# Expert stage of a decoder block: half of the second tile's row sums formed by VectorE in SBUF

## What is computed

```python
def block(args):
    xblk, eblk, gblk = args
    u = u_table[eblk]
    act = jax.nn.gelu(jnp.einsum('nd,nhkd->nhk', xblk, u).astype(jnp.float32), approximate=False) * gblk
    v = v_table[eblk]
    return jnp.einsum('nhk,nhkd->nd', act.astype(v.dtype), v)
...
h = layer_norm(DN_ALPHA * h + peer_ffn(h, w_q_peer[l], sub_keys[l], u_table[l], v_table[l]),
               ln2_g[l], ln2_b[l])
```

## Time and profile before

| | |
|---|---|
| median of three runs | 2472.08 us (2471.37 to 2472.72) |
| profiled execution, first to last instruction (its own time; none besides is given) | 2469.5 us |
| share of the span busy: PE, DVE, ACT, POOL | 89%, 62%, 29%, 27% |
| gathers (software DMA queue) | 537.01 MB of 708.29 MB |
| second tile, about 1800 to 2456 us | DMA at 427 GB/s throughout |
| V gathers of the whole stage, PE matmuls on them | 256, 2032 |

### The profile page before, as it was taken

The page is one execution under the profiler, slowest core; times in us unless marked ns, Lnnn a source line. Parts: engine busy times, 40 slices in busy tenths (PEclk is TensorE's granted clock), DMA queues, the critical chain, the costliest instruction groups (busy, mean ns, idle before and its releaser), DMA issues.

```text
span 2469.5 us, 39419 instructions
## 1 busy us (share of the span) xinstructions
PE 2193.7 (89%) x16183; PEld 1536.9 (62%) x16183; DVE 1533.5 (62%) x2579; ACT 727.0 (29%) x1383; POOL 664.8 (27%) x541
## 2 busy tenths in 40 slices
PE   7999999999999999999989888988787787777776
PEld 6899999999989999988644444533332232222222
DVE  7777777787764554456855776677445544444445
ACT  4555555555434444342211111111111000000000
POOL 1000000000000000002555545555545445444442
PEclk9999999999999999999999999999999999999999
DMA  5433333333347666484999999999999999999997
GB/s 198 137 94 86 100 88 89 97 90 86 97 120 224 184 187 182 139 303 181 404 420 423 423 426 427 427 427 428 427 427 427 426 427 427 427 427 427 427 427 290
DMA packets 346278, 708.29 MB, mean 287 GB/s; under 512 B 13834, under 2 KB 270434, under 8 KB 279778
## 3 DMA queue, kind: packets, MB, share of 16 engines
q0 software_dynamic: 74176, 537.01, 51.7%
q1 hardware_dynamic: 271684, 168.55, 23.3%
q10 hardware_dynamic: 240, 0.22, 0.0%
HBM read 703.63 MB, written 2.10 MB: 286 GB/s over the span
## 4 chain that ended last, share of the span: by engine, by line
DMA 33%; PE 15%; DVE 2%; issue 2%; POOL 1%; DVEq 0%; ACT 0%; POOLq 0%; ACTq 0%
DMA down_rows<-in_v_table,experts 25%; PE bank L1695 11%; DMA up_rows<-in_u_table,experts 8%; PE bank L1611 2%; POOL down_rows L1599 1%; DVE up_rows L1811 0%; PE bank L1638 0%; PE bank L1653 0%; PE bank L1659 0%; ACT diagonal L1755 0%; DVE one_hot L1251 0%; DVE expert_sides L1257 0%; PE bank L1621 0%; PE bank L1665 0%; DVE side_index L1230 0%
## 5 line engine op out<-in xcount | busy, mean ns | idle before, releaser
L1695 PE MATMUL bank<-down_rows,diagonal 128*128 128x512 f32 x2032 | 947.7, 611 | 210.7 <-DMA down_rows<-in_v_table,experts 173.1
L1811 DVE CUSTOM_DVE_ANT_0 up_rows<-up_rows,h 128x2048 f32<-128x2048 f32 x256 | 585.2, 2292 | 523.2 <-DMA up_rows<-in_u_table,experts 523.2
L1695 PEld LDWEIGHTS bank<-down_rows,diagonal 128*128 128x128 f32 x2032 | 375.2, 193 | 741.9 <-issue 385.7
L1593 POOL DMA_INDIRECT up_rows<-in_u_table,experts x256 | 286.0, 1117 | 1207.2 <-POOLq L1269 1091.4
L1599 POOL DMA_INDIRECT down_rows<-in_v_table,experts x256 | 370.3, 1446 | 523.5 <-PE bank L1695 510.5
L182 DVE TENSOR_TENSOR w_half_rest<-w_half,w_half_high 128x1024 fp32r<-128x1024 f32 x224 | 273.0, 1221 | 180.8 <-ACT w_half_high L161 178.9
L197 PE MATMUL project<-hT_high,w_half_high 128*128 128x272 f32 (+1 forms) x1152 | 353.5, 307 | 1.6 <-DVE r L909 1.3
L197 PE MATMUL project<-hT_high,w_half_rest 128*128 128x272 f32 (+1 forms) x1152 | 330.6, 287 | 0.0
L197 PE MATMUL project<-hT,w_half_high 128*128 128x272 f32 (+1 forms) x1152 | 330.0, 287 | 0.0
L161 ACT CAST w_half_high<-w_half 128x1024 fp32r<-128x1024 f32 x224 | 234.7, 1051 | 191.3 <-PE merge_ps L197 122.0
L197 PEld LDWEIGHTS project<-hT_high,w_half_high 128*128 128x128 f32 x1152 | 216.9, 188 | 11.3 <-DVE r L909 1.5
(11 more groups left out here) (338 smaller groups left out, 3013.2 us busy)
## 6 DMA issues: line engine op xcount, KB each, us to landing
w_half<-in_w_in SPq DMA_DIRECT2D x176, 512.0 KB, 4.0
w_half<-in_w_branch_a SPq DMA_DIRECT2D x32, 512.0 KB, 3.9
out_w<-in_w_out SPq DMA_DIRECT2D x16, 1024.0 KB, 5.3
query_w<-in_w_q_peer SPq DMA_DIRECT2D x10, 1024.0 KB, 19.7
w_half<-in_w_branch_b SPq DMA_DIRECT2D x16, 512.0 KB, 3.8
out_w<-in_w_q_peer SPq DMA_DIRECT2D x6, 1024.0 KB, 29.5
up_rows<-in_u_table,experts POOLq DMA_INDIRECT x256, 21.1
down_rows<-in_v_table,experts POOLq DMA_INDIRECT x256, 20.5
```

Source lines behind the costliest of these rows:

```text
L1593: pool.indirect_dma_start(ur[n % RU][:], None, w["u_table"][0], bass.IndirectOffsetOnAxis(ap=k.idx[:, t, h, j:j + 1], axis=0)).then_inc(s_ ...
L1695: mm = nc.tensor.matmul(acc[t][c][:], dg[n % RD][:], vr[n % RV][:, quarter(c)], start=(n == 0), stop=(n == last(t, c)), skip_group_check=True)
L1811: v.tensor_tensor_reduce(ur[n % RU][:], ur[n % RU][:], k.h[:, n // (HEADS * TOPK), :], 1.0, 0.0, ALU.mult, ALU.add, dots[:, n:n + 1]).then ...
```

## The change

In the second tile, columns 1024 to 2047 (quarters 2 and 3) of all 128 slots are added by DVE in SBUF, and PE adds only quarters 0 and 1 of each. The sum of DVE stands in `shared`, the upper half of the tile `rows`. It starts as ALPHA times the token's vector (two instructions behind the first dot of unit 33). From unit 33 on, `share` of slot n stands behind the dot of slot n+4, and the shares of the last four slots stand in `tail`. A share drains the engine, waits for V(n) and issues two instructions of 512 columns each. GpSimd now waits, ahead of V(n) for n from 133 on, for the share of slot n-5 as well as for TensorE's part. The copy of two banks in `tail` is gone.

```diff
-    TAIL = UNIT
...
-        s_tail = k.sem("peer_tail")
+        s_tail, s_shared = k.sem("peer_tail"), k.sem("peer_shared")
+        half = SLOTS // TT
+        shared = rows[:, 2 * 512:D].rearrange("p (c d) -> p c d", d=512)
...
-            return SLOTS // TT * (t + 1) - 1 - (TAIL if t and c > 1 else 0)
+            return half * (t + 1) - 1
...
                         if n >= RV:
                             pool.wait_ge(s_added, n - RV + 1)
+                        if n - RV >= half:
+                            pool.wait_ge(s_shared, n - RV - half + 1)
...
             def begin():
 
-                for n in range(4):
+                for n in range(2):
...
-                    for c in range(4 if n < SLOTS - TAIL else 2):
+                    for c in range(2 if t else 4):
...
+            def share(n):
+
+                d()
+                dve.wait_ge(s_v[n % RV], 16 * (n // RV) + 16)
+                for c in range(2):
+                    ins = v.scalar_tensor_tensor(out=shared[:, c], in0=vr[n % RV][:, quarter(2 + c)], scalar=weights[:, n:n + 1],
+                                                 in1=shared[:, c], op0=ALU.mult, op1=ALU.add)
+                ins.then_inc(s_shared, 1)
+
...
             def tail():
 
+                for n in range(SLOTS - UNIT, SLOTS):
+                    share(n)
+                d()
+                for c in range(2):
+                    v.bn_stats(stats[:, 1, 2 + c, :], shared[:, c])
                 dve.wait_ge(s_out, 16 * 4)
-                dve.wait_ge(s_added, SLOTS - TAIL)
-                for c in range(2, 4):
-                    v.tensor_copy(y[:, quarter(c)], acc[1][c][:])
-                for n in range(SLOTS - TAIL, SLOTS):
-                    d()
-                    dve.wait_ge(s_v[n % RV], 16 * (n // RV) + 16)
-                    for c in range(2, 4):
-                        v.scalar_tensor_tensor(out=y[:, quarter(c)], in0=vr[n % RV][:, quarter(c)], scalar=weights[:, n:n + 1],
-                                               in1=y[:, quarter(c)], op0=ALU.mult, op1=ALU.add)
-                d()
-                for c in range(2, 4):
-                    v.bn_stats(stats[:, 1, c, :], y[:, quarter(c)])
                 dve.wait_ge(s_tail, 2)
...
-                    norm_centre(nc, y[:, quarter(c)], y[:, quarter(c)] if c > 1 else acc[1][c][:], mv[:, 1], gam[:, quarter(c)])
+                    norm_centre(nc, y[:, quarter(c)], shared[:, c - 2] if c > 1 else acc[1][c][:], mv[:, 1], gam[:, quarter(c)])
...
                     if i == 0 and u:
                         weigh(u - 1)
+                    if (u, i) == (PER_TILE + 1, 0):
+                        dve.wait_ge(s_wide, 8)
+                        for c in range(2):
+                            v.tensor_scalar(shared[:, c], k.h[:, 1, quarter(2 + c)], ALPHA, None, ALU.mult)
+                    if u > PER_TILE:
+                        share(UNIT * (u - 1) + i)

```

## The result

The changed kernel takes 2481.67 us (median of 5 runs, 2481.16 to 2482.92) against 2472.08 us before; the ratio is 1.004, with a 95% interval of 1.0027 to 1.0052. It is 0.4% slower, some 9.6 us.

The account below looks back on a forecast made before the run. The second tile was taken as bound by the gathers at 427 GB/s. The sum was 0 (PE) + 0 (DVE) + 3.2 us for one gap at finish(0), 2472.1 + 3.2 = 2475.3 us; range 2471 to 2482 us.

Parts of the forecast that it names:

- rival C: Units 33 to 39: a gather's round trip of 8.2 us leaves zero slack; 2481.9 us, at 8.7 us 2496; chance 0.15.
- The sign that the forecast named: Second tile: DMA at 427 GB/s but for one dip of about 3 us, some 12 us behind finish(0).
- Bound by the gathers at 427 GB/s, the earlier release of the buffers worth nothing: Second tile: DMA always busy, so releasing buffers 1.7 us sooner lands no row sooner; 0 us.
- VectorE's slot of 3.8 us fits in 4.91, 78% busy: Second-tile slots: dot of 2.3 us plus share of 1.46 us leaves 1.1 us to spare; 0 us.
- Four rows in flight, the next U issued at T + 4.1 and needed by T + 12.3: Up to unit 39, T being V(n)'s landing: four rows behind it, U(n+11) lands at T + 9.75, slack 2.55 us.
- The gap at `finish(0)`, 3.2 us: First pass of the first tile's norm: holds the next dot 5.74 us, less slack of 2.55 us.
- The second and third gap, 1.1 and 0.3 us: At finish(1) and finish(2): passes of 3.65 and 2.81 us, each less slack of 2.55 us.
- The output filled the gaps: First tile's 1 MB output behind finish(1) and finish(2), 1.2 us a half, would run inside the second and third gap.
- No loss where the stretch begins: Plain slots from unit 33 on: slack of 2.55 us is enough with four rows in flight; 0 us.
- The clock: TensorE in the second tile: even at 1.2 GHz four matmuls take 3.7 us and fit; 0, at most 1.0 us.
- Rival D: Second-tile slots: GpSimd issues needing time free of VectorE become the bound, 6.2 us a slot; 2630 us; chance 0.03.
- A chance of 0.28 for "slower": Whole kernel: chance of a time more than 0.2% above before, against 0.69 for the same and 0.03 for faster.

Follow-up runs that it names:

- the repetition: The changed kernel itself measured once more, with nothing altered, beside the kernel before on the same chip: 2481.86 us, ratio 1.0046.
- the matched version: Changed kernel with VectorE's shares moved to follow the order in which GpSimd issues the V rows: 2473.15 us, ratio 1.0006.
- the run at clock 1.00: Changed kernel with TensorE doing all four quarters again in the second tile, two into unread banks, except in the last four slots: 2480.37 us, ratio 1.0039.

## Why the prediction was right or wrong

- **The number:** 2481.67 us against a forecast of 2475.3 us. That the range holds it is owed to the part of rival C that it took in, not to the forecast's sum, so it is luck as far as that sum goes. The sign that the forecast named, one dip of about 3 us behind `finish(0)`, came with 5.0 us, and two more behind it.
- **Bound by the gathers at 427 GB/s, the earlier release of the buffers worth nothing:** right. 2000 to 2200 us reads 427 GB/s in every version, and the end of the program lies as far behind the last share as before.
- **VectorE's slot of 3.8 us fits in 4.91, 78% busy:** right, 156.88 of 200 us. The extra load alone costs at most some 0.9 us (ratio 1.0009, an interval that begins at 1.0).
- **Four rows in flight, the next U issued at T + 4.1 and needed by T + 12.3:** right. The trace shows T + 3.9 in plain slots. That it is the mismatch of the two orders is shown by both ways of taking it away (1.0006 and 1.001).
- **The gap at `finish(0)`, 3.2 us: too small.** It is 5.0 us, with no output in it. The part that the sum has was right: U(154) was issued at T + 9.7 and landed 5.5 us later (one issue at 1929.90 us in the repetition's trace, where I had 5.65), and 2.9 us were lost there. I took the DMA to be in full flow again at once, but the three rows behind lost 2.1 us more.
- **The second and third gap, 1.1 and 0.3 us: this step failed.** The run with the output held back shows them alone: 2.5 and 3.7 us. I took the best round trip, 5.65 us, for every pass; it was 5.6, 6.1 and 7.6 us. With these the prediction's own sum (12.3 - 4.1 less the round trip, and the pass less that) gives 3.1, 1.5 and 2.2 us, which is what was lost at the first late U: 3.0, 1.3 and 2.1 us. The three rows behind each, for which the sum has nothing, lost 4.6 us more. Together that is 11.0 us where 4.6 were forecast, 6.4 us more, and the forecast of 2475.3 us was short by 6.4 us. The start of the stretch, 1.6 us, comes on top; the two traces of the changed kernel differ by as much (12.4 and 10.4 us at the passes).
- **The output filled the gaps:** as far as can be told, right. It cost 2.6 us before and added little to gaps that were larger than it needs.
- **Why the later rows take longer** is open. After the first gap the issues stand beside VectorE instructions without a pause: at 1954.59 and 1956.35 us a U and a V issue took 1.46 and 2.56 us, where issues in plain flow take 0.94 and 1.3. But with the sum in PSUM the U issue right behind each pass took 0.94 us, and the gaps were no smaller.
- **No loss where the stretch begins: wrong, but small.** V(127) landed 0.75 us earlier than before and V(143) 0.8 us later, so some 1.6 us went before the first pass. The versions with the passes later and in pieces have it too. U(139), the first row behind the wait for V(128), was issued at T + 3.9 as forecast, but took 9.2 us to land, so it missed T + 12.3 by 0.8 us. Why it took longer wasn't tried.
- **Rival C, the round trip decides:** half right. Plain slots were not stretched: shallow slots without a long pass flow at 424 to 428 GB/s. But its price for the passes with no slack, 12.2 us less 2.4 us for the output, is nearly what was measured, 12.4 less 2.6 us. It reached the sum by another way than the rows took, since the first late U landed in 5.5 us and not in 8.2, and pass by pass the lengths (5.7, 3.7 and 2.8 us) and the gaps (5.0, 3.9 and 3.5 us) differ.
- **Not in the sum at all:** instructions as DMA traffic. VectorE has more of them, TensorE fewer, and only the former's fetches delayed rows. In the matched version it would account for what is left. In the changed kernel it has no visible price: V(155) to V(255) took 472.3 us, against 472.9 us before.
- **The clock:** the cost of 0 was right, and shown by the run at clock 1.00. So the rule of the Trainium skill, page "TensorE: Matmul & The Clock Gate", part 1, that the half clock is the default and activity lifts it, agrees with the 0.69 to 0.78 of the windows against 1.00 with four quarters (155.64 of 200 us busy); it had no price here.
- **Rival D, GpSimd's issues exclude each other with VectorE's:** wrong. Issues do take longer beside VectorE's instructions (2.56 us at 1956.35), but GpSimd never became the bound, and with the sum in PSUM, so one SBUF input in place of two, an issue beside a share took 0.94 us in place of 1.3 and the time was the same. By the rule of the Trainium skill, page "SBUF — State Buffer", section "SBUF: two separate sides", taken as exclusion for the whole of both instructions, a slot would have taken 6.2 us; the late slots take 4.9 at 427 GB/s, so the measurement decides against that reading.

A chance of 0.28 for "slower" was too small: the uncertain prices in the sum (the round trip, the rows behind the first late one, the start of the stretch) were taken at or near their best value, and each of them could only add.

## What to carry to other kernels

When a consumer is put into an engine's program, place it by the order in which the transfers it waits for are issued, and count how many transfers can be in flight while it waits. A stage that is bound by transfers has no spare time in wide blocks: with a deep queue a block of 5.7 us costs nothing, with four rows in flight only what fits into a slot's spare time does, so cut such blocks up or move them. When the queue has run dry, count the rows behind the first late one too. And a round trip taken from an empty, quiet queue is a lower bound: here 5.6 us behind the first pass, but 6.1 and 7.6 us behind the next two.

## What the runs showed of the hardware

An instruction fetch is not free beside transfers that fill the DMA: 8 KB of VectorE's instructions put all later rows off by about 0.8 to 1.0 us (8 fetches, 6.3 us), though 8 KB at 427 GB/s would take 0.02 us. TensorE's fetches (queue 8) in the same stretch left no such mark. That one DMA engine carries the fetch and is also the one whose part of each row lands last would explain it; it was read from the landings and not tested by itself. GpSimd's issue of a gather took 1.3 us beside a VectorE addition with two SBUF inputs and 0.94 us beside the same addition with one of them in PSUM. And TensorE at a granted clock of some 0.75 in place of 1.0 over 600 us cost nothing measurable, since its work still fitted into the slots.
